# A 32-expert layer on one core: merged rows transposed inside the neighbouring products, embedding and second-bias products placed in experts 22 to 27, first expert pieces loaded from the scan on

## The chip, the cores and the metric

The kernel runs on one core of a Trainium2 chip. The metric is the device time of one execution in microseconds (us). Three executions of the kernel before took 1261.02, 1261.99 and 1265.23 us, a median of 1261.99.

## What is computed

One layer of a streaming encoder over 256 tokens of width 1024, all in fp32:

```python
h = rms_norm(x, mix_norm); proj = h @ w_in             # 1024 x 7184: u, v, z, xBC, dt, gate_a, gate_b
y_a = sgu_branch(...)                                  # gated unit
y_b = mamba2_branch(...)                               # convolution, chunked scan ("the scan"), gated norm
merged = sigmoid(gate_a) * (y_a @ w_branch_a) + sigmoid(gate_b) * (y_b @ w_branch_b)
x = x + merged @ w_out
x = x + moe_ffn(rms_norm(x, ffn_norm), ...)            # top 4 of 32 experts, clamped SwiGLU, F = 1024
x = x + sigmoid(rms_norm(x, ple_norm) @ w_ple_gate) * (p @ w_ple_proj)     # embedding p: 256 wide
return rms_norm(x, final_norm)
```

An expert has w1 (1024 x 2048), b1, w2 (1024 x 1024) and b2 (the second bias), 12.6 MB in fp32; the 32 together are 403 MB of the 457 MB that the kernel loads.

## The kernel before, in words

**Engines and order.** Each engine runs its own list of instructions, written out by hand, and the lists meet at semaphores. SP issues all loads, in one order, each behind the waits in front of it. PE is TensorE, ACT ScalarE, DVE VectorE, POOL GpSimd.

**The dense stages.** The products of the layer's first part are made in three fp32r passes each (high times high, high times low, low times high; lines 661 to 663 of `three`). A weight of 1024 x 512 comes as two halves of 1 MB (rows 0 to 511, then 512 to 1023) into four buffers `blk`. SP loads half i when half i-4 has been used (L479); ACT writes its high part (L1100, `split`), DVE its low part (L1404, `weight_low`), and PE multiplies (`natural`: for each block b of 512 output columns, for each half kh, for each of the two tiles t of 128 tokens, 12 matmuls). The order is v, u, z, ga, gb, then `wa` (w_branch_a), `wb` (w_branch_b) and `wo` (w_out). Halves 32 to 35 are those of wb, 36 to 39 those of wo.

**Banks.** The list `unit_order()` names every use of a PSUM bank in order; use i has bank i modulo 8 and waits until the use eight places before has been drained.

**Between wb and wo.** DVE multiplies each wb block by gate_b and adds it to `ga` (L1640, L1642), which gives the merged rows. After the last wb product PE transposes `p` (unit pT), makes three of the four embedding products (units pp, `embed`, L656: p times w_ple_proj, two fp32 matmuls of 128x512 each), and transposes the merged rows (units mT, 16 transposes, L648). ACT and DVE make the high and low parts of mT (L1135, L1397). DVE's list has `weight_low(39)`, the last half of wo, ahead of the low parts of mT. Only when all four mT units are taken does PE begin wo.

**After wo.** DVE adds the wo product to x (L1652), PE transposes x (units fT) and multiplies it with the router's weights (unit logit, L865), then makes the fourth embedding product (L656), the ranks of the tokens within their experts (L891 to L894), the transposed gates (L1004), and gathers the tokens of expert 0 (L902).

**The experts.** Each of the 32 experts takes six pieces of 2 MB ("chunks": four of w1, c0 to c3, then two of w2, c4 and c5), numbered 0 to 191 over the kernel, in a ring of nine slots. Chunks 0 to 8 are loaded ahead (L518); chunk g from 9 on is issued when chunk g-9 has been used (`chunk_used`, L518 up to chunk 11, L571 in a loop of ten rounds of three experts from chunk 12 on). In `expert` PE multiplies c0 to c3 (L940), adds b1 (L948), gathers the next expert's tokens (L902), transposes the activations (L970), scatters the previous expert's result into four banks ACC (L911), multiplies c4 and c5 (L993) and transposes the selection (L918). Expert 0 has no result to scatter; there the second bias of all experts is put into ACC by four matmuls with 32 rows (L978):

```python
                if first:
                    pe.wait_ge(b2_loaded, 16)
                    wait_taken(pe, ("wo", 1, 1), ("logit",), ("pp", 1, 1), ("rank",))
                    for t in range(TT):
                        for dh in range(2):
                            mm(ACC[t][dh][:, :], gateT[:, t * P:(t + 1) * P], b2_all[:, dh * W:(dh + 1) * W],
                               start=True, stop=True)
```

**The end.** PE reads the number of overflow rounds n from memory, skips the overflow branch (n is 0 here), scatters the last result (L1052), transposes x (L1061) and multiplies it with w_ple_gate in three passes (`gate`, L661 to L663), whose high and low parts come from `gate_high` (ACT, L1289) and `gate_low` (DVE, L1769). ACT's table loads, sigmoids (L1327) and squares (L1334) and DVE's products (L1830, L1831) follow; then the result is stored.

## Time and profile before

| what | value |
| --- | --- |
| three executions | 1261.02, 1261.99, 1265.23 us |
| the profiled execution, its own time | 1265.43 us |
| its span, first to last instruction | 1263.5 us |
| PE busy | 1219.7 us (97%) |
| PE weight load busy | 653.8 us (52%) |
| DVE busy | 398.3 us (32%) |
| ACT busy | 222.8 us (18%) |
| POOL busy | 45.0 us (4%) |
| DMA | 457.24 MB, mean 362 GB/s |
| mean granted TensorE clock | 0.984 of full speed |

The time of an execution is the span and some 1.9 us around it. A busy PE is no proof that PE is the bound: its matmuls overlap, and its busy time includes the time that a started matmul takes, not what it waits for in between. Durations below are all of the profiled execution, in us from the start of its span.

### The profile page before, as it was taken

What the parts mean: (1) busy time and instruction counts of PE and PEld (TensorE: products, weight loads), DVE (VectorE), ACT (ScalarE), POOL (GpSimd) and SP (SyncE); (2) the same over time, 40 slices, a digit from 0 to 9 for tenths busy, and PEclk for the clock granted to TensorE, in tenths of its full rate; (3) what the DMA queues carried; (4) which work ended last, traced back from release to release, by engine and by line L of the source; (5) the groups of instructions that cost most, each with busy time, mean ns of one, the idle gap of its engine ahead of it and who ended that gap; (6) DMA issues with size and microseconds to landing.
All of it is one profiled execution on the core that took longest, in us unless ns stands there. A gap on an engine that the chain in (4) does not pass through costs nothing.

```text
span 1263.5 us, 15417 instructions
## 1 busy us (share of the span) xinstructions
PE 1219.7 (97%) x6327; PEld 653.8 (52%) x6327; DVE 398.3 (32%) x716; ACT 222.8 (18%) x313; POOL 45.0 (4%) x32
## 2 busy tenths in 40 slices
PE   8999999989999999999999999999999999999987
PEld 7988788866444444444444444433334443333326
DVE  2769764543111221221122112111112221112126
ACT  4755454442000000000000000000000000000027
POOL 6600000010000000000000000000000000000000
PEclk9989999997999999999999999999999999999999
DMA  9644447937899999999999999999999999999990
GB/s 283 203 141 133 131 149 307 355 138 306 365 429 425 430 428 428 430 427 429 430 426 430 429 427 430 428 428 430 426 430 428 427 430 429 427 430 426 430 364 34
DMA packets 61742, 457.24 MB, mean 362 GB/s; under 512 B 7305, under 2 KB 16881, under 8 KB 37138
## 3 DMA queue, kind: packets, MB, share of 16 engines
q1 hardware_dynamic: 61714, 456.84, 87.9%
q8 instruction: 21, 0.34, 0.1%
q14 instruction: 7, 0.06, 0.0%
HBM read 455.77 MB, written 1.05 MB: 362 GB/s over the span
## 4 chain that ended last, share of the span: by engine, by line
PE 72%; DMA 24%; DVE 2%; issue 1%; ACT 1%; SPq 0%; DVEq 0%; ACTq 0%
PE bank L940 22%; DMA wring<-in_w_dram 18%; PE bank L993 13%; PE bank L902 7%; DMA vz<-in_w_dram 6%; PE bank L661 6%; PE bank L662 5%; PE bank L663 5%; PE bank L911 3%; PE bank L948 1%; PE bank L712 1%; PE bank L719 1%; PE bank L715 1%; PE bank L648 1%; PE bank L970 1%; PE bank L918 1%
## 5 line engine op out<-in xcount | busy, mean ns | idle before, releaser
L940 PE MATMUL bank<-wring,hT 128*64 128x512 f32 x1376 | 309.5, 598 | 12.3 <-DMA wring<-in_w_dram 11.5
L940 PEld LDWEIGHTS bank<-wring,hT 128*64 128x64 f32 x1376 | 95.4, 137 | 206.5 <-issue 177.7
L1743 DVE TENSOR_SCALAR xbcT<-bank 128x512 f32<-128x512 f32 x32 | 22.2, 692 | 436.8 <-PE bank L948 436.8
L993 PE MATMUL bank<-wring,xbcT 128*64 128x512 f32 x688 | 155.9, 601 | 0.6 <-DVE xbcT L1756 0.6
L902 PEld LDWEIGHTS bank<-xbcT,ga 128*128 128x128 f32 x1024 | 121.6, 195 | 3.9 <-DVE xbcT L1706 1.2
L902 PE MATMUL bank<-xbcT,ga 128*128 128x64 f32 x1024 | 120.4, 277 | 0.9 <-DVE xbcT L1706 0.9
L1276 ACT ACTIVATE xbcT<-xbcT 128x512 f32<-128x512 f32 x32 | 20.2, 630 | 512.6 <-DVE xbcT L1743 512.6
L993 PEld LDWEIGHTS bank<-wring,xbcT 128*64 128x64 f32 x688 | 47.9, 138 | 103.7 <-issue 102.9
L1758 DVE COPY xbcT<-bank 128x256 f32<-128x256 f32 x32 | 13.6, 424 | 265.6 <-PE bank L918 265.6
L1404 DVE TENSOR_TENSOR blk_lo<-blk,blk_hi 128x2048 fp32r<-128x2048 f32 x32 | 73.1, 2289 | 53.7 <-ACT blk_hi L1100 53.7
L1281 ACT ACTIVATE xbcT<-bank 128x512 f32<-128x512 f32 x32 | 19.1, 597 | 362.5 <-PE bank L993 362.5
L940 PE MATMUL bank<-vz,hT 128*64 128x512 f32 x336 | 76.4, 597 | 6.2 <-DMA vz<-in_w_dram 6.2
L661 PE MATMUL bank<-blk_hi,a_lo 128*128 128x512 f32 x192 | 77.0, 401 | 2.2 <-issue 2.2
L1100 ACT ACTIVATE blk_hi<-blk 128x2048 fp32r<-128x2048 f32 x32 | 61.3, 1916 | 91.4 <-DMA blk<-in_w_in_dram 50.0
L662 PE MATMUL bank<-blk_hi,a_hi 128*128 128x512 f32 x192 | 76.2, 397 | 0.0
L993 PE MATMUL bank<-blk,xbcT 128*64 128x512 f32 x336 | 76.2, 595 | 0.0
L663 PE MATMUL bank<-blk_lo,a_hi 128*128 128x512 f32 x192 | 76.0, 396 | 0.0
L940 PE MATMUL bank<-blk,hT 128*64 128x512 f32 x336 | 75.9, 593 | 0.0
L911 PE MATMUL bank<-xbcT 64*128 64x512 f32 x248 | 61.6, 615 | 0.0
L940 PEld LDWEIGHTS bank<-vz,hT 128*64 128x64 f32 x336 | 22.7, 137 | 51.8 <-issue 41.1
L993 PEld LDWEIGHTS bank<-blk,xbcT 128*64 128x64 f32 x336 | 23.2, 137 | 49.8 <-issue 49.8
L940 PEld LDWEIGHTS bank<-blk,hT 128*64 128x64 f32 x336 | 23.7, 137 | 48.7 <-issue 45.7
(272 smaller groups left out, 1131.4 us busy)
## 6 DMA issues: line engine op xcount, KB each, us to landing
wring<-in_w_dram SPq DMA_DIRECT2D x129, 2048.0 KB, 33.1
blk<-in_w_dram SPq DMA_DIRECT2D x42, 2048.0 KB, 32.7
vz<-in_w_dram SPq DMA_DIRECT2D x21, 2048.0 KB, 32.9
blk<-in_w_in_dram SPq DMA_DIRECT2D x28, 1024.0 KB, 5.1
blk<-in_w_branch_a_dram SPq DMA_DIRECT2D x4, 1024.0 KB, 5.1
blk<-in_w_branch_b_dram SPq DMA_DIRECT2D x4, 1024.0 KB, 8.7
blk<-in_w_out_dram SPq DMA_DIRECT2D x4, 1024.0 KB, 5.2
x<-in_x_dram SPq DMA_DIRECT2D x4, 512.0 KB, 5.1
```

The source lines that it names most:

```text
L661: mm(out, lhs[1], rhs[0], start=start, stop=False)
L662: mm(out, lhs[0], rhs[0], start=False, stop=False)
L663: return mm(out, lhs[0], rhs[1], start=False, stop=stop)
L902: last = mm(YB[:, k * SLOTS:(k + 1) * SLOTS], xp[:, t, k * P:(k + 1) * P], sel[:, t, :], start=(t == 0), stop=(t == TT - 1))
L911: last = mm(ACC[t][dh][:, :], selgT[dh * SLOTS:(dh + 1) * SLOTS, t, :], y_sb[dh * SLOTS:(dh + 1) * SLOTS, :], start=False, stop=True, skip ...
L940: last = mm(bank[dh * SLOTS:(dh + 1) * SLOTS, :], xgT[:, k, :], at(c)[:, kk * 2 * F + off + dh * W:kk * 2 * F + off + (dh + 1) * W], start ...
L993: last = mm(YB[dh * SLOTS:(dh + 1) * SLOTS, :], actT[:, kk * P + c * SLOTS:kk * P + (c + 1) * SLOTS], at(W1C + c)[:, kk * D + dh * W:kk * ...
L1100: fn(high(i), blk[:, i % NB, :], ACT.Copy).then_inc(blk_high, 1)
L1276: fn(sig_sb, g_sb, ACT.Sigmoid, scale=ALPHA).then_inc(msig_done, 1)
L1281: fn(y_sb, YB[:, :], ACT.Copy).then_inc(y_copied, 1)
L1404: tt(blk_lo[:, i % NB, :], blk[:, i % NB, :], high(i).bitcast(FP32), ALU.subtract).then_inc(nat_low, 1)
L1743: ts(g_sb, GLU[:, :], LIMIT, None, ALU.min).then_inc(g_done, 1)
```

## The change

It does these things. (1) PE transposes the first halves of the merged rows (mT, columns 0 to 511, both tiles) within wb, after the first weight half of its second block, and the second halves within wo, after the first 12 matmuls; wo waits for each mT unit only where it uses it. DVE's and ACT's lists are put in that order, with `weight_low(38, 39)` and the last two `split`s behind the mT parts. (2) The first half of the logits is computed within the last half of wo. (3) pT is transposed behind the logits, and the four embedding products go into experts 24 to 27, into the bank LIN, from which ACT copies them. (4) The second bias is added in experts 22 and 23 instead of expert 0; DVE zeroes ACC at the start. (5) Experts 22 to 30 are written out behind a loop of 21; SP's loop has nine rounds and its last three experts are written out. (6) Chunk 0 is loaded at gb's first half, chunks 1 and 2 where 0 and 1 were, and w_ple_proj (1 MB) at wa's first half and not at wb's. (7) A quarter of w_ple_gate (1 MB) is loaded ahead of the last chunk; ACT makes that weight's second high part (`gate_high(0, 1)`) behind the high parts of x. (8) n is read ahead of expert 31, and the last scatter goes ahead of the overflow branch.

```diff
-    u += [("pT",)] + [("pp", 0, t) for t in range(TT)]
-    u += [("mT", t, h) for t, h in two] + [("pp", 1, 0)] + nat("wo")
+    u += [("mT", t, 0) for t in range(TT)] + [("wo", 0, t) for t in range(TT)]
+    u += [("mT", t, 1) for t in range(TT)] + [("wo", 1, t) for t in range(TT)]
     u += [("fT", t, h) for h in range(2) for t in range(TT)]
-    u += [("logit",), ("pp", 1, 1), ("rank",)]
+    u += [("logit",), ("rank",), ("pT",)]
...
+                if i == HALF_OF["gb", 0, 0]:
+
+                    sp.wait_ge(y_done, TT)
+                    load_chunk(0)
                 if i in (FIRST_WA + 1, FIRST_WA + 3):
 
-                    load_chunk((i - FIRST_WA) // 2)
-                if i == FIRST_WA + NB + 1:
-
-                    sp.wait_ge(y_done, TT)
-                    load_chunk(2)
-                if i == HALF_OF["wb", 0, 0]:
-
-                    sp.wait_ge(yssq_done, TT)
+                    load_chunk((i - FIRST_WA) // 2 + 1)
+                if i == HALF_OF["wa", 0, 0]:
+
+                    wait_filled(sp, ("yaT", 1, 1))
                     load(wpp, w_ple_proj[0].rearrange("(k p) n -> p k n", p=P), wpp_loaded)
...
-            with sp.Fori(0, (E - 2) // GROUP) as i:
+            with sp.Fori(0, (E - 2) // GROUP - 1) as i:
...
+            for g in range(NCH * (E - GROUP), NCH * E):
+                if g == NCH * E - 1:
+
+                    sp.wait_ge(chunk_used, NCH * E - NSLOT + 1)
+                    load_gate(0, 0)
+                sp.wait_ge(chunk_used, g - NSLOT + 1)
+                load_chunk(g)
+            load_gate(0, 1)
...
+            def merged_rows(h):
+
+                for t in range(TT):
+                    pe.wait_ge(merged, TT * h + t + 1)
+                    transposes(("mT", t, h), [ga[:, t, (4 * h + i) * P:(4 * h + i + 1) * P] for i in range(4)])
+
+            def after_wb(b, kh, t):
+                if (b, kh, t) == (1, 0, 1):
+                    merged_rows(0)
+
             wait_taken(pe, *all_of("ybT"))
-            natural("wb", a_hi, a_lo)
...
+            natural("wb", a_hi, a_lo, after=after_wb)
...
+            def after_wo(b, kh, t):
+
+                if (b, kh, t) == (0, 0, 0):
+                    merged_rows(1)
+                if (b, kh, t) == (1, 0, 1):
+                    for r in range(TT):
+                        residual(r, 0)
+                if (b, kh, t) == (1, 1, 0):
+                    pe.wait_ge(wr_scaled, 1)
+                    wait_empty(pe, ("logit",))
+                    for r in range(TT):
+                        logits(r, 0)
+
+            natural("wo", b_hi, b_lo, ready=taken, after=after_wo)
             residual(0, 1)
-            logits(0, 0)
             residual(1, 1)
-            logits(1, 0)
             logits(0, 1)
             logits(1, 1).then_inc(full(("logit",)), 1)
-            embed(1, 1)
+            pe.wait_ge(p_loaded, 16)
+            transposes(("pT",), [p_nat[:, t, k * P:(k + 1) * P] for k in range(2) for t in range(TT)])
...
+            def second_bias(dh):
+
+                pe.wait_ge(b2_loaded, 16)
+                for t in range(TT):
+                    mm(ACC[t][dh][:, :], gateT[:, t * P:(t + 1) * P], b2_all[:, dh * W:(dh + 1) * W],
+                       start=False, stop=True, skip_group_check=True)
+
+            def embed(b, t):
+
+                pe.wait_ge(wpp_loaded, 16)
+                for k in range(PLE // P):
+                    last = mm(LIN[:, :], pT[k][:, t * P:(t + 1) * P], wpp[:, k, b * W:(b + 1) * W],
+                              start=(k == 0), stop=(k == PLE // P - 1))
+                last.then_inc(embed_filled, 1)
...
+            with pe.Fori(0, LOOPED // GROUP) as i:
                 for r in range(1, GROUP + 1):
                     streamed(GROUP * i + r, r, i)
-            streamed(E - 1, E - 1, last_one=True)
-
+            for j in range(LOOPED + 1, E - 1):
+                extra = None
+                if j in BIAS_AT:
+                    extra = lambda: second_bias(BIAS_AT[j])
+                if j in EMBED_AT:
+                    extra = lambda: embed(*EMBED_AT[j])
+                if j - 1 in EMBED_AT:
+                    pe.wait_ge(embed_done, list(EMBED_AT).index(j - 1) + 1)
+                streamed(j, j, extra=extra)
             pe.wait_ge(extra_done, 1)
             n = pe.value_load(n_extra[0:1, 0:1], min_val=0, max_val=OVF - 1)
+            streamed(E - 1, E - 1, last_one=True)
+            pe.wait_ge(y_copied, E)
+            pe.wait_ge(selT_done, E)
+            for t in range(TT):
+                for dh in range(2):
+                    last = mm(ACC[t][dh][:, :], selgT[dh * SLOTS:(dh + 1) * SLOTS, t, :],
+                              y_sb[dh * SLOTS:(dh + 1) * SLOTS, :], start=False, stop=True, skip_group_check=True)
+                last.then_inc(acc_done, 1)
             with pe.If(n > 0):
...
+            merged_high(0)
+            split(HALF_OF["wo", 0, 1])
+            merged_high(1)
+            split(HALF_OF["wo", 1, 0])
+            split(HALF_OF["wo", 1, 1])
...
+            for j in range(LOOPED + 1, E - 1):
+                gated(j)
+                if j in EMBED_AT:
+                    b, t = EMBED_AT[j]
+                    act.wait_ge(embed_filled, list(EMBED_AT).index(j) + 1)
+                    fn(yproj(t, b), LIN[:, :], ACT.Copy).then_inc(embed_done, 1)
                 take_y(j)
...
-            gate_high(0, 1)
             for h in range(2):
                 for t in range(TT):
                     act.wait_ge(tail_filled, TT * h + t + 1)
...
+            gate_high(0, 1)
             gate_high(1, 0)
...
+            weight_low(35)
+            merge(0)
+            weight_low(36)
+            merged_low(0, 12)
+            merge(1)
+            weight_low(37)
+            merged_low(1, 14)
+            weight_low(38, 39)
...
+            for t in range(TT):
+                for dh in range(2):
+                    last = nc.vector.memset(ACC[t][dh][:, :], 0.0)
+            last.then_inc(acc_zeroed, 1)
```

## Rows read from the trace of the kernel before

**Rows 1.** The page's 40 slices: busy tenths of the DMA engines.

```profile
DMA  9644447937899999999999999999999999999990
```

**Rows 2.** The chain that ended last: start us, us, what.

```profile
703.12 13.88 PE bank L940 x64
730.93 13.88 PE bank L940 x64
...
1108.58 3.61 PE bank L940 x16
...
1167.33 3.61 PE bank L940 x16
1171.09 37.38 DMA wring<-in_w_dram
```

**Rows 3.** Windows: us, each engine's busy us, PEclk, DMA share, GB/s.

```profile
268.00:271.40 3.40, 3.40 (x10) 2.63 (x9) 0.00 (x0) 0.91 (x2) 3.32 (x2) 0.51 0.00 0
...
332.90:336.30 3.40, 3.40 (x10) 0.97 (x8) 0.00 (x0) 0.00 (x0) 0.00 (x0) 0.50 0.68 284
1227.20:1230.60 3.40, 3.16 (x8) 1.27 (x8) 0.69 (x1) 0.95 (x2) 0.00 (x0) 0.50 0.41 158
...
315.00:335.80 20.80, 20.80 (x100) 9.75 (x98) 4.33 (x6) 0.63 (x1) 0.00 (x0) 0.93 0.97 401
336.00:340.00 4.00, 4.00 (x20) 1.29 (x18) 0.00 (x0) 0.00 (x0) 0.00 (x0) 0.96 0.32 70
340.00:400.00 60.00, 60.00 (x310) 25.35 (x308) 13.65 (x30) 3.05 (x5) 0.00 (x0) 1.00 1.00 427
```

**Rows 4.** Timeline of SP's DMA issues: chunks 8 to 11, and chunk 13.

```profile
292.40 28.80 SPq L518 DMA_DIRECT2D wring<-in_w_dram  x4
...
337.97 0.34 SPq L571 DMA_DIRECT2D wring<-in_w_dram  x1
```

**Rows 5.** Timeline of PE in expert 0.

```profile
328.81 3.70 PE L978 MATMUL bank<-gb,hT 32*128 32x512 f32 x8
332.43 5.35 PE L993 MATMUL bank<-wring,xbcT 128*64 128x512 f32 x16
```

**Rows 6.** The chain between wb and wo.

```profile
254.96 5.00 DMA blk<-in_w_out_dram
...
261.94 2.29 DVE blk_lo L1404
264.23 1.81 DVE b_lo L1397 x3
...
266.94 0.47 PE bank L661
```

**Rows 7.** Timeline of PE: the 16 transposes of the merged rows.

```profile
260.60 2.03 PE L648 MATMUL bank<-ident,ga 128*128 128x128 f32 x16
```

**Rows 8.** The chain from the end of wo to expert 0.

```profile
291.49 0.44 PE bank L648 x4
...
293.21 2.91 PE bank L865 x24
296.13 3.17 PE bank L656 x4
...
301.23 6.27 PE bank L902 x32
...
308.27 15.99 PE bank L940 x64
```

**Rows 9.** Timeline of DVE: the mask of the four chosen experts.

```profile
297.73 0.23 DVE L1687 TENSOR_TENSOR hT<-hT 128x64 f32<-128x64 f32 x1
```

**Rows 10.** The chain at the end of the experts.

```profile
1225.19 2.26 issue
1227.44 3.54 PE bank L1052 x8
```

**Rows 11.** ACT's timeline near the end.

```profile
1254.99 0.46 ACT L1327 ACTIVATE xbcT<-bank,rstd 128x256 f32<-128x256 f32 x1
```

More of the change, by code:

```diff
@@ L65 @@
 GROUP = 3
+LOOPED = 21
+EMBED_AT = {24: (0, 0), 25: (0, 1), 26: (1, 0), 27: (1, 1)}
+BIAS_AT = {22: 0, 23: 1}
 OVF_SLOTS = (0, 1, 2, 8, 0, 1)
@@ L327, in build @@
         x1_part = sem("x1_part")
+        acc_zeroed = sem("acc_zeroed")
+        embed_filled = sem("embed_filled")
+        embed_done = sem("embed_done")
+        ovf_scattered = sem("ovf_scattered")
         x1_root = sem("x1_root")
@@ L663, in three, with natural @@
                 return mm(out, lhs[0], rhs[1], start=False, stop=stop)
-            def natural(kind, hi, lo, blocks=range(HALVES), between=None):
+            def natural(kind, hi, lo, blocks=range(HALVES), between=None, ready=None, after=None):
                 for b in blocks:
@@ L674, in natural @@
                         for t in range(TT):
+                            if ready is not None:
+                                ready(kh, t)
                             for kk in range(4):
@@ L682, in natural @@
                                 last.then_inc(full((kind, b, t)), 1)
+                            if kh == 0 and t == TT - 1:
+                                last.then_inc(row_half_used, 1)
+                            if after is not None:
+                                after(b, kh, t)
                         if kh == 0:
-                            last.then_inc(row_half_used, 1)
                             if between is not None:
@@ L928, in streamed, with expert @@
                 expert(j, lambda c: slots[(NCH * r + c) % NSLOT], arrived, **kind)
-            def expert(j, at, arrived, first=False, last_one=False):
+            def expert(j, at, arrived, first=False, last_one=False, extra=None, alone=False):
                 pe.wait_ge(xg_done, j + 1)
@@ L971, in expert @@
                 last.then_inc(actT_filled, 1)
-                if first:
-                    pe.wait_ge(b2_loaded, 16)
-                    wait_taken(pe, ("wo", 1, 1), ("logit",), ("pp", 1, 1), ("rank",))
-                    for t in range(TT):
-                        for dh in range(2):
-                            mm(ACC[t][dh][:, :], gateT[:, t * P:(t + 1) * P], b2_all[:, dh * W:(dh + 1) * W],
-                               start=True, stop=True)
+                if first or alone:
+                    pass
                 elif last_one:
@@ L984, in expert @@
                     scatter(lambda: None)
+                if extra is not None:
+                    extra()
                 if not last_one:
@@ L998, in expert @@
                     selected(TB)
+                if alone:
+                    pe.wait_ge(y_copied, j + 1)
+                    pe.wait_ge(selT_done, j + 1)
+                    scatter(lambda: None).then_inc(ovf_scattered, 1)
             pe.wait_ge(gate_done, 1)
@@ L1046, in _ @@
                 with pe.Fori(0, n) as q:
-                    expert(q + E, lambda c: slots[OVF_SLOTS[c]], lambda c: pe.wait_ge(ovf_loaded[c], 16 * q + 16))
-            pe.wait_ge(y_copied, n + E)
-            pe.wait_ge(selT_done, n + E)
-            for t in range(TT):
-                for dh in range(2):
-                    last = mm(ACC[t][dh][:, :], selgT[dh * SLOTS:(dh + 1) * SLOTS, t, :],
-                              y_sb[dh * SLOTS:(dh + 1) * SLOTS, :], start=False, stop=True, skip_group_check=True)
-                last.then_inc(acc_done, 1)
+                    expert(q + E, lambda c: slots[OVF_SLOTS[c]], lambda c: pe.wait_ge(ovf_loaded[c], 16 * q + 16), alone=True)
             for h in range(2):
@@ L1270, in _ @@
             last.then_inc(lexp_done, 1)
-            embed(1, 1)
+            name = ("pT",)
+            wait_filled(act, name)
+            for k in range(PLE // P):
+                last = fn(pT[k], bank_of(name)[:, k * TOKENS:(k + 1) * TOKENS], ACT.Copy)
+            last.then_inc(empty(name), 1)
             fn(table_out[:, 2:3], ones[:, 0:1], ACT.Sigmoid)
@@ L1723, in _ @@
             take_gathered()
+            for t in range(TT):
+                for dh in range(2):
+                    last = nc.vector.memset(ACC[t][dh][:, :], 0.0)
+            last.then_inc(acc_zeroed, 1)
             wait_taken(dve, ("rank",))
```

95 lines of the change are left out of this document (39 added, 56 removed).

## The prediction

> **What bounds the kernel now.** I read the slices first: from the twelfth slice on, the DMA engines are busy at nine tenths or more until the last two slices [rows 1]. That is the stretch of the experts, where PE is busy too, so the chain must say which of the two sets the time. In its first half the chain is PE alone, and an expert takes 730.93 - 703.12 = 27.81 us; in its second half each expert has one DMA piece of some 37 us, and two experts take 1167.33 - 1108.58 = 58.75, or 29.37 each [rows 2]. So PE could do an expert in 27.8, the stream delivers one in 29.4 (six chunks at 4.9 us), and from expert 16 on PE waits for the stream. The end of the experts is therefore where the unbroken stream begins plus a fixed number of chunks. What is done before that point counts in full; PE work after it counts only beyond 1.56 us an expert.
>
> Where does the unbroken stream begin? The windows show chunks 9 to 12 from 315 to 335.8 at a share of 0.97, then 0.32 from 336 to 340, then 1.00 [rows 3]. The gap ends with chunk 13, issued at 337.97 [rows 4], right behind the last matmul of expert 0's first w2 chunk (332.43 + 5.35 = 337.8) [rows 5]. From issue to data it is 2.0 us. Expert 0 begins at 308.27 [rows 8]; call that S. Today the unbroken stream begins at S + 31.7. Two things can move it: an earlier S, and a shorter expert 0.
>
> **From wb to wo.** Today wb's last matmuls are issued at about 254.7 and wo's first at 266.94. In between lie the load of wo's last half (5.00), its high part, its low part (2.29), and only then the last low parts of mT, which stand behind it in DVE's list [rows 6]: 12.2 us. After that, 3.4 us run at PEclk 0.51, which loses half of them, 1.7 [rows 3]. In the changed order PE goes from wb into wo with its high and low parts of mT columns 0 to 511 made 4 us before. What replaces the gap is the 16 transposes, 2.0 us [rows 7]. I went through DVE's new list for what is late next: the second merge ends about 1.5 us after wb, `weight_low(37)` 2.3 later, the low parts of the second mT units about 5 us after wb, and PE wants them 6.3 after. The last half lands 5 us after wb as today, its low part is ready by about 11, and PE wants it at 18. The transposed halves wait for nothing. Gain 12.2 + 1.7 - 2.0 = **11.9 us**. If a wait came back here it would be one low part, 2.3 us; that is my bound on this term.
>
> **From wo to expert 0.** Half of the logits' 32 matmul records, about 1.9 us (24 of them take 2.91) [rows 8], moves into wo: the end of wo moves back by 1.9. Behind wo, today 301.23 - 291.49 = 9.7 us pass to the first gather. Without the first logits, PE's second logits wait a little for the last transposed x; I count 1.2 of the 1.9 as saved. The embedding took 3.17 [rows 8], but 2.0 of it, up to the mask at 297.96 [rows 9], hid DVE's work, so removing it saves 1.2; the exponentials on ACT then come last and give back 0.2. Net: -1.9 + 1.2 + 1.2 - 0.2 = +0.3. **S is 12.2 us earlier**, 296.1. The gather (6.27 [rows 8], slow today) stays as it is. pT's transposes lie in PE's wait for the mask.
>
> **Expert 0.** The bias goes: 3.70 us [rows 5], and with it 3.4 us at a PEclk of 0.50 that begin in the matmuls behind it, 1.7 lost [rows 3]. DVE's copy of the transposed activations, covered by the bias, becomes visible: about 1.0 (an estimate, between 0 and the 3.70 that covered it). So chunk 13 could be issued 4.4 earlier after S, its data at S + 27.3. But chunks 9 to 12 fill the queue until 335.8, S + 27.5 [rows 3]. So the stream is unbroken at about S + 27.7 and not S + 31.7: **4.0 us**. The four memsets on DVE lie beside PE's first four chunks. If the slow clock stays, with another cause than the bias, this is 2.3; if the copy hides, still 4.0.
>
> **Loads ahead.** Chunks 0 to 8 have all landed by expert 1 today as well; chunk 9 waits for a slot in any case. Loading chunk 0 earlier adds 0 by itself. It and the 1 MB of w_ple_proj leave the stretch of wb, which keeps the halves of wb and wo punctual; this supports the first term and is not counted again. SP's new waits are past when it comes to them.
>
> **Experts 22 to 30.** The bias is two matmuls in each of two experts, 3.70 / 2 = 1.85 each; an embedding is two matmuls, 3.17 at the slow clock [rows 8], some 1.7 at full. Together 2 x 1.85 + 4 x 1.7 = 10.5 us. The cover is 1.56 an expert, and PE is short of the stream from about expert 17 on, since both move by the same 16 us. So 0.3 at most is left over in each, 1.4 in all, and experts 28 to 30 take it back. Cost **0**; without the cover, 10.5. The slots are given back up to 2 us later, against a queue of some 35 us. ACT's copy of LIN lies beside c4 and c5. The reading of n ahead of expert 31 falls into a wait for w1 chunks; between 0 and the 2.26 that now stand at the end [rows 10], I take 0.
>
> **The end.** A quarter of the gate's weight ahead of the last chunk delays that by half a chunk, 2.45 us; the last chunk is multiplied second of the w2 chunks and would come just in time, 0 to 0.5. The 2.26 of issue ahead of the last scatter [rows 10] goes, but the branch still stands ahead of the transposes of x. On the other side ACT's 2.6 us of high parts now follow those of x, and ACT is busy up to the last sigmoids today: the one at 1254.99 follows its table load at once [rows 11]. So ACT's list hands on little of PE's gain. I take **0.7**, between -1.5 (ACT's work delays all, less what it waited) and 2.3.
>
> The Trainium skill (Runtime: NRT & Kernel Launch, Instruction fetch mechanics) says that instructions are fetched ahead in sequence, and that a taken branch to a place not yet fetched stops the engine until it is there. By it the 2.26 is the jump, not the reading of n, and goes along with the branch: the last term would be 0 and the sum 16.2.
>
> **Sum.** 12.2 + 4.0 + 0.7 = 16.9 us. Against the profiled execution, 1265.4 - 16.9 = 1248.5; it lies 3.4 above the median shown, and against that it is 1262.0 - 16.9 = **1245.1 us**. The change is worth what it does before the stream is unbroken.
>
> **Rivals.** *The gap in the stream stays* (PE stays slow in expert 0, or the first w2 chunk is late for another reason, or a stall of 2.3 comes back at wo). For it: PEclk is low in several stretches around here, and their cause is only read off. Then 16.9 less 2 to 6: 1247 to 1251. Chance 0.13.
>
> *The extras are not hidden.* The bias's two matmuls fill a quarter of the rows; today slow clock follows them. If each of the six extras brings 3.4 us at half clock [rows 3], the price is 6 x (1.75 + 1.7) = 20.7 against 1.56 x 14 = 22 of cover in experts 17 to 30, of which what lies before expert 22 can't be used, since PE then waits for the stream anyway: 1.56 x 9 = 14. So 6.7 late: 1252. Chance 0.07.
>
> *Slower: code written out stalls PE.* Experts 22 to 30 are straight code where a loop ran. If fetching it cost once per expert what stands at the branch, 2.26, and each such stop brought 3.4 us at half clock as at 1227.2 [rows 3, 10], it would be 9 x 4.0 = 36 with the 10.5 of extras, against 14 of cover: 32 late, **1277**. It decides from (16.9 + 14 - 10.5) / 9 = 2.3 us per expert. Against it: PE's first pass through experts 0 to 3 is new code too, the stream runs beside it, and the chain has no such piece there. Chance 0.04.
>
> The Trainium skill (same page and section) calls the cost of going on to the next block of code mostly hidden; by that this rival falls away.
>
> *Nothing moves*, because the stages before wo are held by a load that I didn't see: within 4 us of before, chance 0.03.
>
> **Numbers.** The forecast has 0.73. Its own spread: 2.3 for a low part, 1.7 for the clock, 2.2 and 1.6 at the end. The range 1241 to 1252 takes in the first two rivals. About 0.3% (4 us) is what a measurement can tell from no change: faster 0.93, same 0.03, slower 0.04.
>
> **What would show it.** Right: no gap between wb and wo; S near 296; DMA share near 1 from S + 7 on; PE still waiting for w1 chunks in expert 31, whose last one begins near 1192 and not 1208.5; expert period 27.8, then 29.4. Wrong: idle PE at L661 within wo; a second stretch of low DMA share after S + 27; no DMA pieces in the chain of experts 28 to 31, which would mean that PE had become the bound; or a gain at S that the last w1 chunk doesn't show.

## The result and the profile after

The changed kernel takes 1253.41 us, the median of five runs (1252.66 to 1255.21), against 1261.99 of before beside it (1260.64 to 1265.23): a ratio of 0.993, 95% interval 0.991 to 0.9949. That is 8.6 us faster where 16.9 were forecast, and outside the range. Repeated on another chip it was 1252.31 against 1262.61, 0.9924 (0.9899 to 0.9949), 9.6 us by the ratio. The direction was right and the size half.

The page's lines of after, to be held against [rows 1]:

```profile
span 1250.8 us, 15307 instructions
...
DMA  9644368777999999999999999999999999999980
...
q8 instruction: 31, 0.51, 0.2%
```

The slices 8 to 10 now read 777 in place of 937, and the eleventh 9 in place of 8; before that, the sixth reads 6 in place of 4, where chunk 0 is now loaded. The last line is the queue that brings code (packets, MB, share of the 16 engines' time): 31 blocks of 16 KB, where before it brought 21.

The chain of after, columns as in [rows 2]: the end of the gather and expert 0, the middle, and the end.

```profile
288.53 7.09 PE bank L925 x32
296.45 16.61 PE bank L963 x64
...
326.12 13.88 PE bank L963 x64
353.94 13.88 PE bank L963 x64
...
948.15 13.88 PE bank L963 x64
...
1067.04 13.88 PE bank L963 x64
1096.76 3.61 PE bank L963 x16
...
1194.52 3.65 PE bank L963 x16
...
1211.39 2.01 PE bank L1075 x8
...
1215.32 1.27 issue
1216.59 3.63 PE bank L1108 x16
```

Expert 0 begins at 296.45, S = 296.1 having been forecast. Without the bias expert 1 (L963 is the old L940) begins 29.7 after S; before it was 33.3. PE alone bounds the experts from 948.15 to 1067.04 (29.72 us each, the extras in them); then PE waits for the stream again, and the last w1 chunk is begun at 1194.52. "Near 1192" was forecast (1208.5 less 16.2): the first 2.2 us of the miss are there.

The windows of after, columns as in [rows 3]:

```profile
288.20:301.90 13.70, 12.54 (x46) 8.82 (x48) 5.91 (x23) 0.00 (x0) 0.00 (x0) 0.50 0.68 290
303.00:323.80 20.80, 19.82 (x110) 9.93 (x108) 4.33 (x6) 0.63 (x1) 0.00 (x0) 1.00 0.97 400
323.80:328.00 4.20, 4.20 (x22) 1.50 (x20) 1.67 (x6) 0.60 (x1) 0.00 (x0) 1.00 1.01 398
328.00:388.00 60.00, 60.00 (x310) 25.39 (x308) 11.97 (x24) 2.45 (x4) 0.00 (x0) 1.00 1.01 428
```

The gap in the stream (0.32 in [rows 3]) is gone: the third row shows 1.01 from S + 27.4 on, and S + 27.7 was forecast. The first row was not foreseen: the gather and the first chunk run 13.7 us at a granted clock of 0.50, the 1.2 GHz level. It is a longer form of something that the kernel before has too, though its rows did not show it: there the granted clock is 0.50 from about 302 to 311, from the gather into the first chunks.

PE's timeline of after, from wb to the gather, columns as in [rows 5] with the idle time before in brackets:

```profile
249.12 1.03 PE L669 MATMUL bank<-ident,ga 128*128 128x128 f32 x8
...
258.17 1.04 PE L669 MATMUL bank<-ident,ga 128*128 128x128 f32 x8
...
286.36 0.41 PE L914 MATMUL bank<-hT,strict 128*128 128x64 f32 x2 [1.51 <-DVE hT L1757]
...
288.53 7.09 PE L925 MATMUL bank<-xbcT,ga 128*128 128x64 f32 x32 [0.89 <-DVE xbcT L1776]
```

The halves of the merged rows are transposed inside wb and wo, without a wait.

### The profile page after: what moved, and what is told of

Same layout as the page of the kernel before. It is cut to its first block, busy times and chain, and to the rows that moved or that the text cites. A ratio compares the mean times of both kernels' runs of the same rounds, so it can differ in the third digit from the quotient of the medians.

```text
span 1250.8 us, 15307 instructions
## 1 busy us (share of the span) xinstructions
PE 1214.9 (97%) x6327; PEld 655.5 (52%) x6327; DVE 400.6 (32%) x720; ACT 222.2 (18%) x314; POOL 45.1 (4%) x32
## 4 chain that ended last, share of the span: by engine, by line
PE 80%; DMA 15%; DVE 2%; ACT 2%; issue 1%; SPq 0%; ACTq 0%; DVEq 0%
PE bank L963 28%; PE bank L1012 15%; DMA wring<-in_w_dram 12%; PE bank L925 8%; PE bank L682 5%; PE bank L684 5%; PE bank L683 5%; PE bank L934 4%; DMA vz<-in_w_dram 3%; PE bank L971 1%; PE bank L738 1%; PE bank L745 1%; PE bank L741 1%; PE bank L993 1%; PE bank L669 1%; PE bank L941 1%
## 5 line engine op out<-in xcount | busy, mean ns | idle before, releaser
L963 PE MATMUL bank<-wring,hT 128*64 128x512 f32 x1376 | 309.3, 599 | 6.8 <-DMA wring<-in_w_dram 6.0
L963 PEld LDWEIGHTS bank<-wring,hT 128*64 128x64 f32 x1376 | 96.8, 138 | 199.1 <-issue 182.9
L963 PE MATMUL bank<-vz,hT 128*64 128x512 f32 x336 | 76.4, 596 | 3.7 <-DMA vz<-in_w_dram 3.7
L963 PE MATMUL bank<-blk,hT 128*64 128x512 f32 x336 | 75.7, 593 | 0.0
L963 PEld LDWEIGHTS bank<-blk,hT 128*64 128x64 f32 x336 | 24.0, 137 | 48.2 <-issue 47.2
L963 PEld LDWEIGHTS bank<-vz,hT 128*64 128x64 f32 x336 | 23.0, 137 | 48.5 <-issue 41.9
```

Source lines behind the costliest of these rows:

```text
L963: last = mm(bank[dh * SLOTS:(dh + 1) * SLOTS, :], xgT[:, k, :], at(c)[:, kk * 2 * F + off + dh * W:kk * 2 * F + off + (dh + 1) * W], start ...
```

## The experiments

**One anchor for all traces.** The first matmul with dt's 16 columns comes early in the program, ahead of all that was changed. It starts anywhere from 58.77 to 61.63 us, and from 58.77 to 61.52 in three traces of the kernel before alone. So the distances are more telling than the times: S less this anchor; the last w1 chunk of expert 31 less S, and less the start of expert 1; the end of the span less that chunk. The last column counts the blocks of code that the code queue moved.

| kernel | anchor | S less anchor | last w1 less S | last w1 less expert 1 | end | blocks of code |
| --- | --- | --- | --- | --- | --- | --- |
| before | 59.13 | 249.1 | 900.2 | 866.9 | 54.9 | 21 |
| before_again | 58.77 | 247.2 | 898.9 | 866.5 | 55.2 | 21 |
| before_third | 61.52 | 246.0 | 900.0 | 866.7 | 55.0 | 21 |
| lists_order | 61.20 | 241.4 | 898.1 | 866.8 | 54.8 | 21 |
| after | 58.88 | 237.6 | 898.1 | 868.4 | 56.2 | 31 |
| after_again | 58.83 | 237.5 | 897.7 | 868.2 | 56.3 | 31 |
| no_extras | 60.63 | 237.5 | 897.9 | 868.5 | 56.0 | 31 |
| gate_first | 61.28 | 237.6 | 898.1 | 868.3 | 55.2 | 31 |
| loop_all | 60.97 | 237.6 | 896.3 | 866.8 | 54.6 | 21 |
| unroll18 | 59.40 | 236.5 | 899.6 | 870.9 | 52.1 | 41 |
| bias_back | 60.79 | 237.6 | 901.9 | 868.3 | 56.5 | 31 |
| no_branch | 61.63 | 236.2 | 897.3 | 868.3 | 51.3 | 29 |
| first18 | 61.43 | 237.6 | 901.2 | 871.5 | 51.3 | 41 |
| short3 | 61.16 | 237.6 | 897.8 | 868.1 | 55.4 | 28 |
| loads_old | 60.81 | 238.8 | 896.9 | 868.2 | 56.7 | 31 |
| two_paths | 61.51 | 236.5 | 898.0 | 869.3 | 51.4 | 31 |

S less anchor is not free of chance either: a stretch of 3.4 us at half clock near 131 us, ahead of all that was changed, is missing in before_third, unroll18, no_branch, loads_old and two_paths, and where it is missing the first transposes of the merged rows come 1.6 us sooner behind the anchor (before and before_third: 195.6 and 194.1 for those of p); in loads_old another stretch before it is 3.4 us longer and takes that back.

**Both kernels again** (before_again, after_again, before_third: no edit).

> The kernel before, once more, for a second trace of it. The profiled execution on which the prediction rests took 1265.4 us, 3.4 above the median of 1262.0. Theory A (part of what I counted as gain is not in every execution): this trace lacks some of the stretches at half the TensorE clock that the first one had at 268.0, 332.9 or around expert 0, and expert 0 begins up to 2 us earlier; its own time is then nearer 1261. Theory B (the spread lies elsewhere): the same stretches at the same places, expert 0 at 308.3 again, and the difference in time in the stream of the experts.

> The changed kernel, once more. Its first trace had expert 0 at 296.45, the last w1 chunk of expert 31 at 1194.5 and 1252.7 us in all. Theory A: the slow stretches of its start vary by up to 2 us and the rest follows it one to one, 1252.5 to 1255.5. Theory B: expert 0 at 296.4 within 0.3, and a difference in time, if there is one, in the stream of the experts.

> The kernel before, a third trace. If the slow stretches at 295.3 and 332.9 of the first trace are the exception, expert 0 takes 32.4 us as in the second trace and begins some 243.5 us behind the program's first slow stretch, not 245.1; its span is near 1260 to 1262. If they are the rule: 33.3 us and 245.1.

Before: medians 1264.39 (12 runs, 1257.76 to 1268.06) and 1262.39 (10 runs). Before's S less anchor is 249.1, 247.2, 246.0, while of the twelve traces with the new prologue eight lie at 237.5 or 237.6, three at 236.2 to 236.5 (those without the stretch near 131), and only loads_old apart. Of the expectations, before_again bore out theory A (two stretches fewer, S 2.3 sooner, its own time 1262.08), after_again theory B (S at 296.36), and before_third stands between: the stretch at 332 is there again, the one at 295 is not. The chain of before_again, from the gather on:

```profile
299.69 5.55 PE bank L902 x32
...
306.01 16.74 PE bank L940 x64
...
327.38 3.63 PE bank L978 x8
331.00 7.02 PE bank L993 x32
```

L902 took 6.27 in [rows 8] and 5.55 here; the stretch at half clock from 295.3 that the first trace has is missing in the two others. The windows of before_again at the places of two of the first trace's slow stretches, 295.3 and behind the bias:

```profile
295.30:298.70 3.40, 3.22 (x17) 1.76 (x16) 2.58 (x19) 2.25 (x6) 0.00 (x0) 1.00 0.98 419
...
332.90:336.30 3.40, 3.40 (x18) 1.15 (x16) 0.00 (x0) 0.00 (x0) 0.00 (x0) 1.00 0.48 145
```

The granted clock is 1.00 in both, and 18 matmuls pass in the second where 10 did in [rows 3]. The trace that I predicted from had more slow stretches than either of the two others. Two it shares with both: the one in wo (268.0 in [rows 3]), and the one from the gather on, about 10 us long, from 301 or 302 to 311. Against that trace S less anchor falls by 11.5, against the mean of the three (247.5) by 9.9.

**lists_order**: the kernel before, with the new order in DVE's and ACT's lists alone.

```diff
-            split_ahead("wo", 0)
             high_parts("mT", b_hi)
+            split_ahead("wo", 0)
...
-                if t == 0:
-                    weight_low(35 + 2 * b, 36 + 2 * b)
+                if (b, t) == (0, 0):
+                    weight_low(35, 36)
...
-            weight_low(39)
             low_parts("mT")
+            weight_low(37, 38, 39)
```

> The kernel before with nothing but the order of two lists changed: DVE makes the low parts of wo's last three halves behind those of the merged rows, and ACT splits wo's last half behind their high parts. PE's list is as before, so the transposes stay behind two embedding products. My reading of the gap of 12.2 us between wb and wo: merging would end 5 us sooner, the transposes stay where they are (they follow the products), and wo begins 3 us sooner, a gap of about 9; the time falls by 2 to 4 us. Rival (the gap is the load of wo's last half): no change, since that load ends when it did.

1258.66 (10 runs), 0.9974 (0.9953 to 0.9995), 3.4 us faster. PE's timeline of lists_order around the gap:

```profile
256.87 0.60 PE L648 MATMUL bank<-ident,xbcT 128*128 128x128 f32 x4
...
266.65 0.47 PE L661 MATMUL bank<-blk_hi,b_lo 128*128 128x512 f32 x1 [0.49 <-issue]
```

From pT's transposes to wo it is 9.8 us; in before_again it is 266.71 - 254.41 = 12.3. So 2.5 of the gap were nothing but the order of these two lists (`weight_low(39)` ahead of the low parts of mT foremost; the run moves the others with it); the rest needs the transposes moved. Two slow stretches of before are gone in this trace as well. The one in wo: from wo's first matmul to the first late transposes of x it is 16.4 us, 18.1 in before. And the one from the gather on, as the chain of lists_order shows:

```profile
298.03 3.80 PE bank L902 x32
```

The same 32 matmuls took 6.27, 5.55 and 6.37 in before's traces. So S less anchor is 241.4, 6.1 below the mean of before, though the medians differ by 3.4 only (0.6 to 5.9 by the interval).

**loads_old**: the changed kernel, with chunks 0 to 2 at their old places.

```diff
-                if i == HALF_OF["gb", 0, 0]:
-                    sp.wait_ge(y_done, TT)
-                    load_chunk(0)
-                if i in (FIRST_WA + 1, FIRST_WA + 3):
-                    load_chunk((i - FIRST_WA) // 2 + 1)
+                if i in (FIRST_WA + 1, FIRST_WA + 3, FIRST_WA + NB + 1):
+                    load_chunk((i - FIRST_WA) // 2)
```

> The changed kernel with chunks 0, 1 and 2 loaded where the kernel before loads them (at the second and fourth half of wa and the second of wb). The prediction gave this part 0. Then expert 0 begins at the same distance from the start of the program within 0.3 us. Rival (the 2 MB ahead of wb's halves make PE wait in wb or wo): PE idles ahead of a half of wb, and expert 0 begins 1 to 5 us later.

1253.14 (5 runs), 0.9922 (0.9895 to 0.9948): no difference from after. S came 1.2 later by the anchor and the last w1 chunk 1.2 sooner behind S, so that chunk stands at 1135.6 or 1135.7 behind the anchor in both. About half of the 1.2 comes in wb, where PE now waits 0.43 us for the merged rows (not at all in after); the slow stretch from the gather on begins sooner and so ends sooner in expert 0, and that gives it back. "Adds 0 by itself" held by the time, though not, as I had expected, with S unmoved, and in part by the luck of where that stretch fell.

**bias_back**: the changed kernel with the second bias in expert 0 again.

```diff
-                if first or alone:
+                if first:
+                    pe.wait_ge(b2_loaded, 16)
+                    pe.wait_ge(acc_zeroed, 1)
+                    for t in range(TT):
+                        for dh in range(2):
+                            mm(ACC[t][dh][:, :], gateT[:, t * P:(t + 1) * P], b2_all[:, dh * W:(dh + 1) * W],
+                               start=False, stop=True, skip_group_check=True)
+                elif alone:
                     pass
...
-                if j in BIAS_AT:
-                    extra = lambda: second_bias(BIAS_AT[j])
```

> The changed kernel with the whole second bias back in expert 0. Prediction's term: the bias costs expert 0 2.7 us net (3.7 less the 1.0 that it covers) and 1.7 more if 3.4 us at half clock follow it, and the stream is broken again ahead of chunk 13, so the last w1 chunk of expert 31 comes 2.3 to 4.0 us later after the start of expert 0 than 897.9. Rival (the stream is bound elsewhere): below 1 us later.

Windows of bias_back:

```profile
323.40:326.80 3.40, 3.40 (x10) 0.97 (x8) 0.00 (x0) 0.00 (x0) 0.00 (x0) 0.51 0.65 275
...
326.00:330.00 4.00, 4.00 (x18) 1.25 (x16) 0.00 (x0) 0.00 (x0) 0.00 (x0) 0.89 0.35 66
```

The half clock behind the bias and the hole in the stream both come back, and the last w1 chunk moves by 901.9 - 898.1 = 3.8 us. My step said 4.0. All of it lies in expert 0: from the start of expert 1 on the distance is 868.3, as without the bias. The whole kernel, 1255.16 (5 runs), 0.994 (0.9919 to 0.9961) lies 1.8 to 2.9 above the medians of after, not clear of the spread.

**no_extras** leaves out the four embedding products, their copies on ACT and the second bias; experts 22 to 30 stay written out. **loop_all** leaves out the same and runs experts 1 to 30 in the loop, on PE and on ACT.

```diff
-                if j in BIAS_AT:
-                    extra = lambda: second_bias(BIAS_AT[j])
-                if j in EMBED_AT:
-                    extra = lambda: embed(*EMBED_AT[j])
...
```

```diff
-LOOPED = 21
+LOOPED = 30
```

> The changed kernel without the four embedding products, their copies and the two halves of the second bias, which are left out of the result; experts 22 to 30 still written out. Theory A (PE work of 1.9 us an expert against 1.56 of cover delays the last chunk): the last w1 chunk of expert 31 begins 1.0 to 2.0 us earlier than with them, and the time falls by as much. Theory B (the stream itself is slower there, with the code that is fetched beside it): no change within 0.5 us, and two experts still take more than 58.75 us between waits. The prediction had 0 for the extras.

> The changed kernel without embedding products and second bias (left out of the result) and with experts 1 to 30 of PE and 1 to 30 of ACT back in loops. The last run without them but with experts 22 to 30 written out took 897.9 us from the start of expert 0 to the last w1 chunk of expert 31, as with them, and its waits between experts 22 and 31 stood up to 60 us apart for two experts instead of 58.7. Theory A (fetching the written-out code takes DMA time from the stream, some 0.16 us a block of 16 KB): 1.6 us less, 896.2, and 58.7 us for two experts throughout. Theory B (the later quarter of the gate's weight or SP's written-out loads cost it): 897.9 again.

no_extras: 1254.11 (11 runs), 0.9934 (0.9914 to 0.9954), no faster than after. The extras cost nothing, and the theory that they did falls. loop_all: 1249.56 (4 runs), 0.9894 (0.9868 to 0.992). The chain of no_extras:

```profile
959.34 3.65 PE bank L963 x16
...
1018.39 3.65 PE bank L963 x16
...
1078.19 3.65 PE bank L963 x16
...
1196.10 3.65 PE bank L963 x16
```

and that of loop_all:

```profile
960.00 3.65 PE bank L963 x16
...
1018.73 3.65 PE bank L963 x16
...
1077.46 3.65 PE bank L963 x16
...
1194.92 3.65 PE bank L963 x16
```

In both, PE waits for the stream at each of these places, so they show the stream's own pace. Looped, four pairs of experts take 1194.92 - 960.00 = 234.9; written out, 1196.10 - 959.34 = 236.8. The written-out code makes the stream 1.8 us slower over eight experts, and it does so with no work added. The quarter of the gate's weight ahead of the last chunk and SP's written-out loads stand in both, so they are not the cause.

**unroll18** (the changed kernel with 18 experts written out, `LOOPED = 12`), **first18** (the same, with gate_first's edit below) and **short3** (gate_first's edit; both biases in expert 22, two embeddings each in 23 and 24, and 25 to 30 in a loop of two rounds). The lines below are short3's.

```diff
+            streamed(LOOPED + 1, LOOPED + 1, extra=both_biases)
+            streamed(LOOPED + 2, LOOPED + 2, extra=lambda: both_embeds(0))
+            pe.wait_ge(embed_done, 2)
+            streamed(LOOPED + 3, LOOPED + 3, extra=lambda: both_embeds(1))
+            pe.wait_ge(embed_done, 4)
+            with pe.Fori(0, 2) as i:
+                for r in range(LOOPED + 4, LOOPED + 7):
+                    streamed(GROUP * i + r, r, i)
```

> The changed kernel with experts 13 to 30 written out instead of 22 to 30; the result is complete. Theory A (code written out costs the stream): the last w1 chunk of expert 31 comes at 899.5 to 900 us after the start of expert 0, 1.5 to 2 us later than 897.9, and two experts take over 59 us from expert 13 on where PE waits for the stream. Theory B: 897.9, no change.

> Two edits of the changed kernel together: ACT's gate part ahead of x's high parts, and experts 13 to 30 written out. Alone they gave 55.2 and 52.1 us from the last w1 chunk to the end, against 56.3, and 898.1 and 899.6 us for the experts before it. Theory A (the jump is cheap here because its target has been fetched already, and ACT's list then bounds the end): 51 to 51.5 us for the end, as without the branch at all. Theory B (in the run with 18 experts the short end came from something else that goes with it): 52 us or more. The stream costs 1.6 us more than with 9 experts written out in either case.

> The changed kernel with ACT's gate part first and with only experts 22 to 24 written out: both halves of the second bias in 22, two embedding products each in 23 and 24, into LIN and GLU; experts 25 to 30 in a loop. The result is complete. By the stream theory (0.16 us per block of code fetched, about one block per expert): 6 to 7 fewer blocks, the last w1 chunk 1.0 us earlier, 896.9 after the start of expert 0. The extras are 3.8 us an expert against 1.56 of cover, 6.7 in sum, and the six experts behind give back 9.4, so they cost nothing. Rival (the doubled extras do delay the last chunk): later than 898.1. The end 55.2 us, or 51.3 if the place of the branch in the code happens to be a good one.

Last w1 less S: 899.6 and 901.2 with 41 blocks of code, against 898.1 with 31 and 896.3 with 21; 897.8 with 28. From 21 to 41 that is 3.3 to 4.9 us, 0.17 to 0.25 a block. Measured from expert 1 on, behind the slow stretch whose place varies, the traces fall into narrow groups: 866.5 to 866.9 in all five with 21 blocks, before's included; 868.1 to 868.5 with 28 to 31 (two_paths apart, see below); 870.9 and 871.5 with 41. That is 1.6 us for the first ten blocks and 2.6 to 3.1 for the next ten. first18 lost twice what I had set for it (3.1, not 1.6), unroll18 2.6 by the distance from expert 1, and short3 saved only three blocks, so little came back. Its experts 22 to 24 were 31.4 us long each:

```profile
951.94 13.88 PE bank L963 x64
983.38 13.88 PE bank L963 x64
1014.82 13.88 PE bank L963 x64
```

That is 3.6 beyond 27.8 in each, and still the last chunk does not move: PE makes it up in the experts behind them, and the stream does not run dry. Medians 1249.63 (4 runs, 0.9912, 0.9881 to 0.9943), 1251.97 (4 runs, 0.9907, 0.987 to 0.9943) and 1253.17 (5 runs, 0.9907, 0.9876 to 0.9938). unroll18's 1249.6 is not owed to the stream but to the end, which shrank from 56.2 to 52.1.

**The end: gate_first, no_branch, two_paths.** gate_first puts ACT's first high parts of the gate's weight back ahead of those of x:

```diff
+            gate_high(0, 1)
             for h in range(2):
...
-            gate_high(0, 1)
```

no_branch is gate_first without the reading of n and without PE's overflow branch (its body does not run on these inputs). two_paths keeps both, and takes the branch ahead of expert 29:

```diff
+            def last_experts():
+                for j in range(E - GROUP, E - 1):
+                    written_out(j)
+                streamed(E - 1, E - 1, last_one=True)
+                ...
             with pe.If(n > 0):
+                last_experts()
                 ...
+            with pe.Else():
+                last_experts()
```

> The changed kernel with ACT's second high part of the gate's weight back ahead of the high parts of x, where the kernel before has it. Theory A (ACT's list is the bound of the end, and the 2.6 us now stand in it behind x, while ACT idles 6.4 us before): ACT begins the remaining high parts 2.5 us earlier, the last sigmoid waits for PE again, and the time falls by 1.0 to 2.5 us. Theory B (the data of that part comes too late, so that x's high parts wait behind it): no gain, or up to 1 us more.

> The changed kernel with ACT's gate part ahead of x's high parts and without PE's reading of n and PE's overflow branch (which is never taken with these inputs; overflow rounds are left out). Theory A (the 3.2 us of idle between the last scatter and the transposes of x are the jump over the branch): the idle falls to below 1 us and the transposes begin 2.5 us sooner after the last w1 chunk; the time falls by 0.5 to 2 us against the same kernel with the branch, less than the idle since ACT's list bounds the end. Theory B (the idle is DVE's additions to x): no change.

> The changed kernel with ACT's gate part first, and with PE's overflow branch taken ahead of expert 29: experts 29 to 31 and the last scatter stand twice in PE's list, once ahead of the overflow rounds and once for the case without them, so that no jump lies between the last scatter and the transposes of x. The result is complete. Theory A (the stall belongs to the jump): the transposes follow the scatter at once, the end takes 51.3 us and not 55.2; the jump's 3.2 us ahead of expert 29 are covered by PE's waits for chunks (1.56 an expert over three experts), and the last w1 chunk stays within 0.5 us of 898.1 after the start of expert 0; in sum 3.5 to 4 us less than the same kernel without the move. Rival (two jumps cost twice, one at the end of the list's first copy as well): the end still has 3 us of idle, no gain.

PE's timeline of gate_first, and then of two_paths:

```profile
1213.79 1.99 PE L1075 MATMUL bank<-xbcT 64*128 64x512 f32 x8 [0.70 <-ACT xbcT L1331]
...
1218.98 3.53 PE L1108 MATMUL bank<-ident,x 128*128 128x128 f32 x16 [3.20 <-issue]
```

```profile
1212.89 1.99 PE L1077 MATMUL bank<-xbcT 64*128 64x512 f32 x8 [0.70 <-ACT xbcT L1342]
1214.81 0.66 PE L1119 MATMUL bank<-ident,x 128*128 128x128 f32 x4
```

With the branch between the scatter and the transposes of x, PE stands 3.20 us at "issue", and its 16 transposes then take 3.53. With the branch elsewhere the first four follow at once, and all 16 are through 2.7 us after the first began, a wait of 0.20 among them. Where it went, in the chain of two_paths:

```profile
1097.10 13.88 PE bank L963 x64
...
1124.91 2.60 issue
1127.51 15.54 PE bank L963 x64
...
1195.96 3.65 PE bank L963 x16
```

2.60 of issue and 1.7 of slow clock, ahead of an expert in which PE has time. It was not quite free there: from expert 1 on the last w1 chunk comes after 869.3 us and not 868.3, with two blocks of code more beside the stream, so of the 3.9 that the end gains some 2.9 remain. The end is 51.3 in no_branch and 51.4 in two_paths against 55.2 in gate_first: the branch costs 3.9. I had expected up to 2 of it. How much of that is the slow clock, loop_all shows: PE stands 3.09 us at the same jump, but no stretch at half clock follows, the 16 transposes take 1.97, and its end is 54.6 against 56.0 in no_extras, 1.4 less. gate_first's own edit is worth 1.0 to 1.1 (55.2 against 56.2 and 56.3). ACT's timeline in after and then in gate_first:

```profile
1217.74 0.60 ACT L1364 ACTIVATE b_hi<-bank 128x512 fp32r<-128x512 f32 x1 [6.41 <-PE bank L1108]
...
1220.74 2.55 ACT L1339 ACTIVATE pg_hi<-vz,paramT 128x512 fp32r<-128x512 f32 x4
```

```profile
1214.16 2.56 ACT L1339 ACTIVATE pg_hi<-vz,paramT 128x512 fp32r<-128x512 f32 x4 [0.42 <-issue]
...
1219.99 0.60 ACT L1365 ACTIVATE b_hi<-bank 128x512 fp32r<-128x512 f32 x1 [3.27 <-PE bank L1108]
```

In after ACT is idle for 6.41 us and makes these high parts of the gate's weight only behind x's; in gate_first they fill part of that idle time.

Medians: gate_first 1251.39 (7 runs), 0.9918 (0.9888 to 0.9948); no_branch 1248.68 (4 runs), 0.9892 (0.9867 to 0.9918); two_paths, which computes everything, 1250.32 (6 runs), 0.9894 (0.9876 to 0.9911), 12 us below the 1262.26 of before beside it. Its median is 2.0 to 3.1 below those of after and its trace 3.0 to 3.4 shorter; the intervals of the ratios just overlap, so that it beats the changed kernel rests on the end, 51.4 for 56.2, which its trace shows; 1.0 of that is gate_first's edit.

## Why the prediction was half right

Four steps failed: that the 2.26 of issue goes from the end and ACT's list costs little; that code written out costs nothing unless PE stalls, a term that was left out; that the gather "stays as it is"; and that one trace, 3.4 us above the median, can stand for the kernel. Taken between the anchor and the end, with the mean of before's three traces and the two of after:

| term | forecast | shown |
| --- | --- | --- |
| S | 12.2 | 247.5 - 237.6 = 9.9 |
| stream behind S | 4.0 | 899.7 - 897.9 = 1.8 |
| end | 0.7 | 55.0 - 56.2 = -1.2 |
| sum | 16.9 | 10.5 |

The measured ratios give 8.8 and 9.6, with intervals to 11.4 and 12.7; start-ups that differ by up to 3 us from one execution to the next are in them.

**S: the size was off by 2.3.** The mechanism held: the gap from wb to wo is gone, and S fell at 296.45. The sum "12.2 + 1.7 - 2.0" held too: the gap was 12.1 to 12.3 in before's traces, the slow stretch in wo is in all three and in none with the new prologue, and against its own trace the gather begins 242.1 - 229.7 = 12.4 us sooner behind the anchor, 12.2 forecast. The step that failed is "The gather (6.27, slow today) stays as it is": it took 7.09, for the stretch at half clock that begins around it is 13.7 us long in after and about 10 in before, where it begins 1 us into the gather. That is 0.8 to 0.9. The rest is the base: the first trace's 249.1 lies 1.7 above the mean of the three, 0.85 of it by the stretch at 295.3 that the other two lack, 0.5 by the one near 131 that before_third lacks, 0.2 by the gather. Why the clock is low from the gather on is not settled. PE had small waits ahead of it in both kernels (1.51 and 0.89 in after, 0.18 and 0.89 in before_again); the stretch is in all three traces of before and in all twelve with the new prologue, and in lists_order, with 0.18 and 0.90, it is not.

**The sum was taken from the wrong base.** Worked out on an execution 3.4 us above the median, and full of its extra losses, it was subtracted from the median unchanged. Of the extra losses I named the size and then dropped them. Even against its own trace the sum was too large: that span fell by 1263.5 - 1250.8 = 12.7, not 16.9.

**Expert 0 was right.** bias_back puts 3.8 back where 4.0 was forecast; expert 1 begins 3.6 sooner after S than in the first trace (3.4 against the mean of the three, of which before_again lacks the slow stretch behind the bias), chunk 13 meets a full queue, and the share stays at 1.01.

**Extras at 0 were right**, and the rival that priced them at half clock was wrong: no_extras gains nothing, though each of the six takes 1.91 us, 11.5 in all and not 10.5. **Loads at 0 were right** by the time (loads_old). Two side sums of the prediction are off and change nothing: with the slow clock left in, expert 0's term would be 31.7 - 29.0 = 2.7 and not 2.3, and what the extras leave over adds up to 1.1 and not 1.4.

**The written-out code was a term I did not have.** My rival asked whether it would stall PE, and left out that code comes through the DMA engines that bound these experts. It cost 1.6 to 1.8 of the stream (loop_all against no_extras), 4.1 to 4.7 from expert 1 on for twice as many blocks. With it, the last w1 chunk less S fell by 3.4 - 1.6 = 1.8 and not by 4.0. The sign of "slower: code written out" was right and its place wrong: PE never shows a stall there, and the price is a twentieth of the 36 us. That the code is the cause is shown; that its blocks delay the data on the DMA engines is my reading. Ten blocks more are 0.17 MB (0.51 for 0.34 in the page's third section), 0.4 us at the 428 GB/s of these experts; by the time of its packet a block takes 6.7% of the 16 engines for 1 us, so ten take 0.7 us, less than half of what is lost. In unroll18 the data queue had also moved 0.9 MB more than in loop_all when the last w1 chunk began (448.66 for 447.78), 2 us of the stream: data of later loads went ahead of the chunk that PE waited for. How the order comes to change was not tried. The Trainium skill (Runtime: NRT & Kernel Launch, Instruction fetch mechanics) calls the fetching of code in sequence mostly hidden. For PE the trace agrees; for a saturated stream the runs differ, and the measurement decides.

**The end was wrong by 1.9.** The step that failed is "The 2.26 of issue ahead of the last scatter goes": the stall stayed with the branch, now 3.22 us long. The Trainium skill's rule on a taken branch (same page and section), that it stops the engine until the place it goes to has been fetched, would have it so, and that rule I had weighed and not taken. In after, before, gate_first and loop_all the trace agrees: one block of code is moved within the idle time. By it the last term would have been 0. The term came out as a loss of 1.2, since the half clock behind the stall slows the transposes of x (3.61 for 2.7), where before it slowed the last scatter (3.53 for 1.99), and ACT's list, re-ordered, costs 1.0 to 1.1. The value lies near my lower bound of -1.5.

In unroll18 and first18 the branch stands where it stood in the list, and no stall shows:

```profile
1212.35 1.99 PE L1075 MATMUL bank<-xbcT 64*128 64x512 f32 x8 [0.70 <-ACT xbcT L1331]
1214.27 0.66 PE L1108 MATMUL bank<-ident,x 128*128 128x128 f32 x4
```

In unroll18 a block was moved at 1208, 4 us ahead of the scatter, and none between it and the transposes; so what lies behind the branch seems to have been brought already. Where in the code the branch falls then decides, and a shift of the code by nine experts won 3.9 us (51.3 for 55.2).

## What to carry to other kernels

Before a sum of small terms is worked out, take the kernel's trace two or three times and measure from a point ahead of all that is changed; slow-clock stretches that one trace alone shows are not the kernel's. Look at the order of each engine's own list before moving work between stages: two lists put in another order were worth 3.4 us by themselves here. A conditional jump belongs ahead of work that has time to spare, even if that work must then be written twice, and not between the last products and the tail. Where the DMA stream was the bound, code in a loop was cheaper than code written out, so write out only the rounds that differ.

## What the hardware showed that I had not expected

- The same list of early work reaches its first dt matmul between 58.77 and 61.63 us: 2.9 us of an execution are settled before the changed part begins.
- At the jump over the branch PE stood 2.3 us (before) to 3.6 us (loads_old) in thirteen traces, and not at all in unroll18 and first18. In before [rows 3, 10], after, gate_first and two_paths a stretch at the 1.2 GHz level followed it, 3.4 us long, in loop_all none; the stall alone (3.20) was less than the whole price, 3.9 us.
- The bias's matmuls with 32 rows were followed by 3.4 us at half clock in bias_back, lists_order and two of before's three traces, not in before_again; in after no stretch at half clock stands between expert 1 and the end of expert 31.
- Each further block of 16 KB of code cost the saturated stream 0.16 us from 21 to 31 blocks and 0.26 to 0.31 us from 31 to 41, while its own packet takes about 0.07 us of the 16 engines' time.
